# Two-layer attention and mixture-of-experts block: how far the last layer's scores run ahead, and where one 2 MB weight load stands in the queue

## The reference

```
for layer in range(2):
    zx, zc = modulate(rms_norm(x)) @ w_in, modulate(rms_norm(h_ctx)) @ w_in
    # four head groups: MLA softmax attention (4 heads), windowed attention with a sink (4),
    # differential attention (4 heads, two softmaxes each), multi-scale pooling
    ox = latent_mix(...) @ w_out
    x = x + gate1 * rms_norm(ox)
    if layer == 0: h_ctx = the same for the context tokens
    fx = hier_moe(modulate(rms_norm(x)))     # top-1 of 4 groups, top-2 of its 4 experts
    x = x + gate3 * rms_norm(fx)
    if layer == 0: h_ctx = the same
return x
# hier_moe: 16 experts, each w_gu (1024 x 1024) and w_down (512 x 1024)
```

## Time and profile before

| | us |
|---|---|
| median of three executions | 1147.26 (1145.5 to 1150.52) |
| the profiled execution: its own time | 1145.34 |
| its span in the profile | 1143.5 |
| TensorE busy | 969.3 (85%) |
| VectorE busy | 311.7 (27%) |
| ScalarE busy | 269.1 (24%) |
| GpSimd busy | 189.7 (17%) |
| moved by DMA | 313.67 MB, mean 274 GB/s |

### The profile page before, as it was taken

How to read it: one execution, slowest core, us unless ns; L and a number is a source line. 1 busy time by engine, 2 the same in 40 slices (tenths; PEclk the granted TensorE clock), 3 DMA queues, 4 the chain that set the end, 5 groups by cost and what they waited for, 6 DMA issues and landing times. The chain is left out here.

```text
span 1143.5 us, 24736 instructions
## 1 busy us (share of the span) xinstructions
PE 969.3 (85%) x9692; PEld 594.1 (52%) x9693; DVE 311.7 (27%) x868; ACT 269.1 (24%) x716; POOL 189.7 (17%) x312
## 2 busy tenths in 40 slices
PE   3999999999899487887899718999989778898786
PEld 2354646455455365654567416676655445554343
DVE  2100035555523611111111132004672511111013
ACT  4121024355422200100010145103562210000002
POOL 0010015000004221111122120002300322232111
PEclk9999999999999699999999958999999799998788
DMA  9983527657743679999989965423113769999992
GB/s 375 365 265 111 221 80 288 253 211 265 268 190 142 258 275 400 369 423 425 401 351 383 417 240 199 139 81 148 74 40 115 294 273 403 425 429 429 428 429 92
DMA packets 56423, 313.67 MB, mean 274 GB/s; under 512 B 12282, under 2 KB 20516, under 8 KB 37796
## 3 DMA queue, kind: packets, MB, share of 16 engines
q1 hardware_dynamic: 36480, 280.00, 60.8%
q0 software_dynamic: 7152, 24.58, 6.2%
q10 hardware_dynamic: 12724, 8.14, 2.3%
HBM read 304.24 MB, written 14.75 MB: 279 GB/s over the span
## 5 line engine op out<-in xcount | busy, mean ns | idle before, releaser
L949 PE MATMUL psum<-weights,lat 128*32 128x256 f32 x2688 | 161.9, 393 | 40.0 <-DVE lat L1794 15.4
L949 PEld LDWEIGHTS psum<-weights,lat 128*32 128x32 f32 x2688 | 100.8, 113 | 95.4 <-issue 54.7
L566 PE MATMUL psum<-hT,weights 128*128 128x512 f32 (+1 forms) x336 | 121.7, 522 | 4.7 <-ACT lat L1144 3.2
L566 PEld LDWEIGHTS psum<-hT,weights 128*128 128x128 f32 x336 | 65.4, 196 | 58.6 <-issue 48.8
L972 PE MATMUL psum<-weights,lat 128*32 128x256 f32 x1344 | 82.8, 383 | 8.9 <-ACT lat L1321 5.4
L1312 ACT ACTIVATE lat<-psum 128x128 f32<-128x128 f32 x64 | 17.8, 278 | 287.9 <-PE psum L949 229.2
L1794 DVE TENSOR_TENSOR lat<-lat,psum 128x128 f32<-128x128 f32 x64 | 23.7, 370 | 205.3 <-ACT lat L1312 205.3
L723 PE MATMUL psum<-weights,R 128*128 128x64 f32 x480 | 65.0, 275 | 10.0 <-ACT R L1223 9.4
L1534 DVE TENSOR_REDUCE st<-psum 128x1 f32<-128x512 f32 (+1 forms) x96 | 55.2, 596 | 65.3 <-PE psum L702 38.2
L723 PEld LDWEIGHTS psum<-weights,R 128*128 128x128 f32 x480 | 59.9, 193 | 16.2 <-ACT R L1223 15.2
L972 PEld LDWEIGHTS psum<-weights,lat 128*32 128x32 f32 x1344 | 49.6, 111 | 35.8 <-issue 14.5
(11 more groups left out here) (304 smaller groups left out, 1277.0 us busy)
## 6 DMA issues: line engine op xcount, KB each, us to landing
weights<-in_exp_w_gu_dram SPq DMA_DIRECT2D x44, 2048.0 KB, 15.0
weights<-in_ada_w_dram SPq DMA_DIRECT2D x24, 2048.0 KB, 7.4
weights<-in_exp_w_down_dram SPq DMA_DIRECT2D x22, 2048.0 KB, 15.0
hT<-in_exp_w_gu_dram SPq DMA_DIRECT2D x10, 2048.0 KB, 11.7
R<-in_exp_w_gu_dram SPq DMA_DIRECT2D x10, 2048.0 KB, 14.0
spare_w<-in_exp_w_down_dram SPq DMA_DIRECT2D x10, 2048.0 KB, 13.0
weights<-in_w_in_dram SPq DMA_DIRECT2D x6, 2048.0 KB, 12.2
weights<-in_w_out_dram SPq DMA_DIRECT2D x4, 2048.0 KB, 7.8
```

Of the source, the lines that this page charges most:

```text
L566: mm = nc.tensor.matmul(t[:, lo:hi], w[:, k, col:col + P], hT[:, k, lo:hi], start=(k == 0), stop=(k == KD - 1))
L949: mm = nc.tensor.matmul(gu_ps[BLK * j:BLK * j + BLK, 0:256], (xgT if L < LAST else xgT_last)[:, k, :], w[:, k % 4, j, :, :], start=(k == 0 ...
```

## The change

The last layer gets `ahead` = 4 as well, so it needs a fifth buffer for probabilities. It takes `hT[:, 0, :]`, one eighth of `hT`. The piece `lo` of expert 2 (2 MB, all of `hT`) can therefore not be loaded during attention. Its load is moved behind the last unit's values, right after `dn` of expert 0. The first layer keeps its buffers and its order.

```diff
-        prob = [part(R1, i * NTOK, NTOK) for i in range(3)] + [part(spare_w, 0, NTOK), part(W[0], EXP_W - NTOK, NTOK)]
+        fifth = [part(W[0], EXP_W - NTOK, NTOK), hT[:, 0, :]]
+        probs = [[part(R1, i * NTOK, NTOK) for i in range(3)] + [part(spare_w, 0, NTOK), fifth[L]] for L in range(DEPTH)]
...
         def ahead(L):
-            return 4 if L < LAST else 3
+            return 4
...  (turn, softmax and weigh use probs[L][...] for prob[...])
                     sp.wait_ge(*at("used", hi - 3))
                     load_piece(L, 1, 1, "lo")
-                    load_piece(L, 2, 2, "lo")
...
                 for piece in PIECES if L < LAST else ("dn",):
                     load_piece(L, 0, 0, piece)
+                if L == LAST:
+
+                    load_piece(L, 2, 2, "lo")
                 for n in (hi - 2, hi - 1):
                     sp.wait_ge(*at("used", n))
```

More of the change, by code:

```diff
@@ L709, in turn @@
                     for i in range(4 if qt < 2 else 2):
-                        mm = nc.tensor.transpose(t[:, i * P:(i + 1) * P], prob[u % (ahead(L) + 1)][:, i * P:(i + 1) * P], ident)
+                        mm = nc.tensor.transpose(t[:, i * P:(i + 1) * P], probs[L][u % (ahead(L) + 1)][:, i * P:(i + 1) * P], ident)
                     mm.then_inc(*mark(S, ("filled", "pT", L, u)))
@@ L1209, in softmax @@
                             act.wait_ge(*at("prob", L, other[-1]))
-                        a((prob[u % (ahead(L) + 1)] if v == 0 else prob2)[:, 0:nk], read(act, "s", L, u, v)[:, 0:nk], ACT.Exp,
+                        a((probs[L][u % (ahead(L) + 1)] if v == 0 else prob2)[:, 0:nk], read(act, "s", L, u, v)[:, 0:nk], ACT.Exp,
                           bias=s_[:, v:v + 1], accum_out=s_[:, 2 + v:3 + v])\
@@ L1556, in weigh @@
                         v.wait_ge(*at("c1", L, u))
-                        stt(prob[u % (ahead(L) + 1)][:, 0:nk], prob2[:, 0:nk], s_[:, 6:7], prob[u % (ahead(L) + 1)][:, 0:nk], ALU.mult, ALU.add)\
+                        stt(probs[L][u % (ahead(L) + 1)][:, 0:nk], prob2[:, 0:nk], s_[:, 6:7], probs[L][u % (ahead(L) + 1)][:, 0:nk], ALU.mult, ALU.add)\
                             .then_inc(*mark(S, ("prob", L, u)))
```

## The result

The changed kernel takes 1154.37 us in the median of 20 runs (1150.45 to 1163.23); the kernel before took 1148.24 in 20 runs beside them (1143.22 to 1154.1). The ratio is 1.0057 [1.0042, 1.0073]: about 6.5 us slower, where the prediction had +1.4 and "no change" as its likeliest case. The profiled execution took 1152.48 us with a span of 1150.7. In the kernel after, lines from 243 on have numbers one higher: 711, 724, 1224 and 1570 are the former 710, 723, 1223 and 1569.

A forecast was written before the change was run, and what follows sets the result against it. DMA bounds the last expert stage, whose start hangs on attention, where TensorE is nearly full. Terms +0.3 - 0.1 + 1.2 + 0 = +1.4 us on the 1147.26 median gave 1148.7 us, range 1144.0 to 1153.0.

The forecast's parts named there:

- no change: Whole kernel: a shift under 0.5% (5.7 us) either way, which can't be told from none; chance 0.86.
- The rival of the clock: TensorE's clock fall, at 896 to 898 between two query tiles' logits, shifts elsewhere: -1.6 to +3 us, chance 0.16.
- Part 1, the loop: Attention: scores, maxima, exponential, copy, values stay one step long whatever the distance; no gain on eight waits totalling 4.1 us.
- Part 2, the start: Start of attention: the copy for the first values moves behind the exponentials of unit 4; a loss of 0.3 us.
- Part 3, the MLA merge: Merge of MLA outputs: the bank wait stays at about 1.4 us, a later copy wait shrinks; -0.1 us in sum.
- Part 4, the end of the steps: End of attention: pooling matmul and diff merge uncovered plus a projection gap, +1.6; VectorE's sums give back 0.4; sum +1.2 us.
- Part 5, the load: Behind attention: expert 2's moved piece fits into DMA rest and VectorE's idle time covers the row's 3.6 us delay; cost 0.
- The rivals of the load and of the row: Moved piece delays the expert stream by 5.0 us, chance 0.07; `amp2_row` lands past its 4.08 us cover, +0.9, chance 0.15.
- the waits go: Attention: the deeper setting removes the short copy waits and the merge wait, up to -5.3 us; chance 0.12.

The follow-up runs named there:

- The exchange on ScalarE: Kernel before, three units ahead, with ScalarE's copy of the transposed probabilities put ahead of its exponentials in the last layer: 1143.54 us, ratio 0.9958.
- the distance alone: Changed kernel with only the four units ahead: fifth buffer in spare_w, expert 2's load at its old place; 1156.52 us, ratio 1.0071 to the kernel before.

## Why the prediction was wrong

**The step that failed is the clock.** The prediction took it as at its upper level "all through attention", priced every longer pause at its own length, and let the clock move only behind attention. Measured: of +6.28 in attention, +2.2 is there at full clock (86.27 with the pauses filled, against 84.06) and 4.1 is the clock (90.34 against 86.27). These are single executions; the medians say about the same (1.0057 to 1.0012, about 5 us). That the pauses matter is shown by filling all of them: the falls go. That filling helps in another way is excluded by the kernel before with its pauses filled (0.999). The one pause of 1.65 us added to the kernel before, with a fall behind it, points the same way, but the pause of 1.59 in the kernel before with pooling in step 24 brought none. So the pauses are a cause of the falls, and which of them brings one is open. The rival of the clock named the right mechanism, with up to +3 us, but at the wrong place.

**Part 1, the loop: right.** Predicted, no gain on the eight waits; measured, eight waits, 4.6 for 4.1. The one that grew is at the start (part 2); the others are at most 0.65. The exchange on ScalarE confirms the loop: the copy behind the exponentials was what closed it. The Trainium skill ("Perfetto Trace Analysis", section "Optimization Strategy") says that a gap repeating on the engine that should be saturated can mean too few buffers. In this case it did not: a fifth buffer left the gaps (4.6 us for 4.1), another order on ScalarE removed them.

**Part 2, the start: right.** From the first scores (791.64) to the point where the same work is done, which is behind the scores of unit 5 in the kernel before (801.20) and behind the first values in the kernel after (804.36), 9.56 became 9.93, +0.37 for +0.3. That this loss stands in one pause of 1.30 was not given a price.

**Part 3, the MLA merge: small miss.** The wait stays, at 1.48 (forecast: about 1.4), and as forecast it now stands before the swa scores of step 16. From the scores of step 15 to those of step 20 the stretch at full clock went from 14.76 to 15.04 (in the kernel with pooling back in step 23, whose clock stays up there), +0.28 for -0.1. A new wait of 0.48 there, for the exponential of the unit whose bank the next scores take, was not foreseen.

**Part 4, the end of the steps: right in kind, a little small.** The uncovered pooling matmul and the gap (0.56 for 0.4) cost +1.92 in the kernel with the distance alone and +1.59 in the kernel before with pooling in step 24, for +1.6 (from the scores of step 23 to the projection). The stretch before it, steps 20 to 23, got 0.24 shorter, for the 0.4 that VectorE's sums were to give back. In sum +1.7 for +1.2, inside its bounds (0.4 to 1.8).

**Part 5, the load: right.** Cost 0; the row lands 12.5 us after its issue (forecast 12 to 14), 2.7 later and not 3.6:

```profile
R<-vec_out POOLq DMA_DIRECT2D x1, 512.0 KB, 12.5
```

```profile
897.54 1.28 DVE L1653 SCALAR_TENSOR_TENSOR R<-x_tok,rs,R 128x1024 f32<-128x1024 f32 x1 [5.92 <-DMA R<-vec_out]
...
901.00 0.75 DVE L1640 SCALAR_TENSOR_TENSOR R<-psum,rs,R 128x512 f32<-128x512 f32 x1 [1.58 <-issue]
```

1.58 us of cover are left, where about 0.5 was forecast. The rivals of the load and of the row didn't come; neither did "the waits go".

**The sum.** At full clock +2.3 in place of +1.4 (0.37 + 0.28 + 1.68), close to the +2.2 of the kernel with its pauses filled. This alone would have been within the predicted range; the 4 us of the clock took it out. (One more us of the distance between 1148.7 and 1154.37 is not the change: the kernel before had a median of 1148.24 in the runs beside it, for the 1147.26 that the prediction started from.)

**What stays open.** What exactly keeps the clock up. The six profiled executions of kernels four units ahead with some or all pauses unfilled all show a fall in attention, the two with all pauses filled none; of the six with three units ahead only the one with the added pause does. The length of a pause alone doesn't decide: the clock stayed up behind 1.59 (861.20 in the kernel before with pooling in step 24), behind 1.47 (837.83 in the kernel with pooling in step 23) and behind 1.30 (803.41 in the kernel after). And with one or two places filled the clock fell elsewhere, once at 820 to 832 with the last pause before it 1.07 us long, and in the kernel after a second time behind pauses of 0.43 and 0.33. Only one execution of each kernel has a trace, so how often a given pause brings a fall isn't known. Not tried: the exchange on ScalarE with filled pauses, which would show whether the fourth unit is worth something once the loop is open.

## What to carry to other kernels

Before going deeper, find the loop that a repeated short wait closes: if it is one step long on every engine in it, another buffer moves nothing, and the order of two operations on the engine that is waited for is worth more (here 4.6 us for two moved lines). Where TensorE is nearly full, price a lengthened pause above its own length, since work behind it may run at half the clock. When steps are shifted, list what hangs on the step number; work that lay in a wait (here a matmul of 1.03 us) may come to stand in the open.

## What the runs showed of the hardware

TensorE's clock can fall inside a stretch in which the engine is busy for over 90% of the time (83.27 of 90.34 us in the kernel after): a pause of 1.65 us was followed by a fall, one of 1.59 in another kernel was not, and a kernel with pauses of at most 1.3 and 1.48 us lost about 4 us of its 6.5 to it. The place differs between executions of the same code (first at about 834 in the kernel after, at about 806 in the one with the pooling matmul in step 23, which is the same up to there). By the Trainium skill ("TensorE: Matmul & The Clock Gate", section "Part 1: The HAM clock gate") the clock follows how busy the engine has been lately, and the same kernel can measure differently from run to run; both agree with these traces. 45 matmuls that nobody needs cost less than they gave back in the changed kernel, whose ratio went from 1.0057 to 1.0012; 36 of them in the kernel before, whose clock doesn't fall in attention, gave nothing (0.999 [0.9971, 1.0009]).

A transfer of 512 KB to 128 partitions on GpSimd's queue lands 11.4 to 12.5 us after its issue in the six kernels in which two weight pieces are under way on SyncE's queue, and 8.6 to 9.8 us after it in the eight with one (the earlier trace rows for the kernel before).
